# A copy of V into unit order during the mixing stage, and whole-row loads in the V stage

## The reference, cut to what matters

```python
q = einsum('bsd,dhe->bshe', h, w_q)             # 8 heads, two halves of 128
s1, s2 = (q halves) . k1, k2                    # 128 scores a side
top_s, ids = best 16 of the 16 x 16 sums        # experts out of 128*128 = 16384
gates = softmax(top_s)
act = gelu(einsum('td,thkd->thk', h, u[ids]))   # u: (16384, 1024)
out = einsum('thk,thkd->td', gates * act, v[ids])  # v: (16384, 1024)
```

## Time and profile before

| what | value |
|---|---|
| median of the timed runs | 1936.13 us |
| the profiled execution, its own time | 1935.26 us |
| its span in the profile | 1933.3 us |
| PE busy | 1852.7 us, 96% of the span |
| DVE / ACT / POOL busy | 1277.3 / 754.3 / 1135.8 us |
| moved by transfers | 360.89 MB, mean 187 GB/s |

### The profile page before, as it was taken

One profiled execution on the slowest core, in us unless ns is written; L12 is line 12 of the kernel. 1 busy time (PEld: TensorE's weight loads), 2 busy tenths in 40 slices (PEclk: granted clock), 3 DMA queues, 4 the chain that ended last, 5 costly groups with the idle time before them and its releaser, 6 DMA issues.

```text
span 1933.3 us, 24277 instructions
## 1 busy us (share of the span) xinstructions
PE 1852.7 (96%) x9045; PEld 1611.5 (83%) x9045; DVE 1277.3 (66%) x2244; ACT 754.3 (39%) x1190; POOL 1135.8 (59%) x666
## 2 busy tenths in 40 slices
PE   6999999989999999999999999988899989999987
PEld 5777788878888888888888888888899989989976
DVE  6355422357899778888989860137686867787543
ACT  5433322333232344444444442433343434344331
POOL 6322344433354476766767764478888888886420
PEclk9999999989999999999999999999999999999998
DMA  5211122312244435544454546649999999999501
GB/s 195 79 66 66 57 99 95 120 66 88 93 146 149 145 124 211 185 174 174 181 202 174 176 173 240 219 161 317 324 344 335 316 350 331 322 344 374 175 33 44
DMA packets 186484, 360.89 MB, mean 187 GB/s; under 512 B 16384, under 2 KB 122880, under 8 KB 184704
## 3 DMA queue, kind: packets, MB, share of 16 engines
q1 hardware_dynamic: 142304, 231.76, 35.8%
q0 software_dynamic: 22528, 67.19, 9.4%
q10 hardware_dynamic: 21536, 60.40, 8.4%
HBM read 298.44 MB, written 60.82 MB: 186 GB/s over the span
## 4 chain that ended last, share of the span: by engine, by line
PE 74%; POOL 17%; issue 3%; DMA 3%; DVE 2%; ACT 1%; ACTq 0%; SPq 0%; DVEq 0%
PE bank L744 36%; PE bank L552 11%; PE bank L554 10%; PE bank L553 10%; POOL wl L491 7%; POOL picked L519 6%; PE bank L769 2%; DMA raw<-stream 2%; POOL rows_ex L526 2%; POOL gout L526 1%; POOL rows_h L526 1%; PE bank L648 1%; PE bank L668 1%; PE bank L722 1%; PE bank L638 0%
## 5 line engine op out<-in xcount | busy, mean ns | idle before, releaser
L491 POOL TENSOR_TENSOR wl<-raw,wh 128x1024 fp32r<-128x1024 f32 x298 | 737.9, 2478 | 670.8 <-ACT wh L846 669.6
L846 ACT ACTIVATE wh<-raw 128x1024 fp32r<-128x1024 f32 x338 | 356.6, 1056 | 324.4 <-PE bank L554 269.1
L552 PE MATMUL bank<-hh,wh 128*128 128x512 f32 (+1 forms) x1056 | 394.5, 374 | 26.4 <-DVE x L1399 17.5
L744 PE MATMUL bank<-hh,wh 128*128 128x512 f32 x1024 | 400.5, 391 | 0.8 <-ACT scores L1001 0.8
L744 PE MATMUL bank<-hh,wl 128*128 128x512 f32 x1024 | 401.0, 392 | 0.0
L744 PE MATMUL bank<-hl,wh 128*128 128x512 f32 x1024 | 399.7, 390 | 0.0
L554 PE MATMUL bank<-hh,wl 128*128 128x512 f32 (+1 forms) x1056 | 387.7, 367 | 0.0
L553 PE MATMUL bank<-hl,wh 128*128 128x512 f32 (+1 forms) x1056 | 387.4, 367 | 0.0
L552 PEld LDWEIGHTS bank<-hh,wh 128*128 128x128 f32 x1056 | 201.3, 191 | 56.0 <-DVE x L1399 19.4
L744 PEld LDWEIGHTS bank<-hh,wl 128*128 128x128 f32 x1024 | 192.2, 188 | 37.7
L744 PEld LDWEIGHTS bank<-hl,wh 128*128 128x128 f32 x1024 | 192.4, 188 | 36.9
(11 more groups left out here) (211 smaller groups left out, 2569.7 us busy)
## 6 DMA issues: line engine op xcount, KB each, us to landing
raw<-stream SPq DMA_DIRECT2D x338, 512.0 KB, 3.7
score_dram<-gout ACTq DMA_DIRECT2D x128, 256.0 KB, 2.5
gate_dram<-stage ACTq DMA_DIRECT2D x12, 2048.0 KB, 7.5
gate<-gate_dram SPq DMA_DIRECT2D x16, 1536.0 KB, 12.7
score_in<-score_dram SPq DMA_DIRECT2D x64, 384.0 KB, 10.5
x<-xT SPq DMA_DIRECT2D x4, 512.0 KB, 5.6
picked<-score_dram,score_at POOLq DMA_INDIRECT x128, 6.1
outT<-outb SPq DMA_DIRECT2D x8, 256.0 KB, 2.1
```

The source lines that it names most:

```text
L491: nc.gpsimd.tensor_tensor(wl[:, n % SL, :], raw[:, n % RAW, :], wh[:, n % SL, :].bitcast(F32), ALU.subtract).then_inc(lo_done, 1)
L552: nc.tensor.matmul(out, ah, bh, start=start, stop=False)
L744: last = nc.tensor.matmul(psum[u % 2][:], w(weights, U_DENSE + u, c), tokens[c][:, :], start=c == 0 and which == 0, stop=c == DC - 1 and w ...
L846: nc.scalar.activation(wh[:, n % SL, :], raw[:, n % RAW, :], ACT.Copy).then_inc(hi_done, 1)
```

## The change

The kernel gets a new tensor in device memory, `v_units`, with 128 tiles in the order and shape of the V units. During units 6 to 69 SP issues two copies from `stream` to `v_units` ahead of each load, 128 copies of 512 KB in all. They wait for nothing. The first load of the V stage waits for all copies, and each V unit is then loaded from `v_units` as 128 rows of 4 KB.

```diff
+        v_units = nc.dram_tensor("v_units", (NK, P, UW), F32, kind="Internal").ap()
+        v_copied = sem("v_copied")
...
+            def copy_unit(m):
+
+                g, dp, hb = m // GB, m % GB // 2, m % 2
+                first = U_V0 + GB * g + HB * hb
+                part = stream[first:first + HB, :, 2 * P * dp:2 * P * (dp + 1)]
+                sp.dma_start(v_units[m].rearrange("p (j d) -> p j d", j=HB), part.rearrange("j p d -> p j d")).then_inc(v_copied, 16)
+
             for n in range(N_UNITS):
                 m = n - U_V0
+                for k in range(NK):
+                    if U_MIX + 2 + k // 2 == n:
+                        copy_unit(k)
...
                 if n >= RAW:
                     wait_low(sp, n - RAW)
+                if n == U_V0:
+                    sp.wait_ge(v_copied, 16 * NK)
                 if U_V0 <= n < U_PLE:
-                    g, dp, hb = m // GB, m % GB // 2, m % 2
-                    first = U_V0 + GB * g + HB * hb
-                    part = stream[first:first + HB, :, 2 * P * dp:2 * P * (dp + 1)]
-                    sp.dma_start(raw[:, n % RAW, :].rearrange("p (j d) -> p j d", j=HB),
-                                 part.rearrange("j p d -> p j d")).then_inc(raw_in[n % RAW], 16)
+                    sp.dma_start(raw[:, n % RAW, :], v_units[m]).then_inc(raw_in[n % RAW], 16)
                 else:
                     sp.dma_start(raw[:, n % RAW, :], stream[n]).then_inc(raw_in[n % RAW], 16)
```

## The result

The changed kernel takes 1941.76 us, the median of 20 runs (1938.67 to 1947.48), against 1936.66 for the kernel before on the same chips (20 runs, 1930.96 to 1939.76). The ratio is 1.0027, with a 95% interval of 1.0019 to 1.0034: 5.1 us slower by the medians, just over the 0.2% bound. The direction is as forecast. The size is not (12 us were forecast), and its terms are further off than the total, because the costs and the gain were both forecast too high and partly cancel.

A forecast was written before the change was run, and what follows sets the result against it. PE was taken to bound the merge stage; in the V stage transfers were short, with POOL nearly as short. 1935.3 + 9.6 (start) + 7.6 (norm) + 2 (clock) - 7 (V stage) = 1947.5, say 1947 us; 8-in-10 range 1925 to 1992.

The forecast's parts named there:

- The cost of a copy: SP's queue: c, the time of all 16 engines for one 512 KB copy, 1.5 to 2.9 us, taken as 2.4.
- the first rival: Copies overlap reading and writing, c of 1.5 to 1.9: 1929 to 1933 us, say 1931; chance 0.28.
- the start: Start of mixing: loads up to unit 10 stand behind ten copies, so PE is 9.6 us late at c = 2.4.
- the norm: Last square before the norm: loads of units 36 to 62 fall behind copies, delay 52c - 117.2, 7.6 us at c = 2.4.
- the 7 us of the V stage: V stage: loads of 4 KB rows save 11 to 15 us of transfer time, of which 7 us come through.
- its own signs of being wrong: U stage starting at its old place (c below 1.9) or over 50 us later, or V stage shrinking by over 18 us.
- the cover of 3.9 us: Start of mixing: slack between ACT's rounding of unit 10 with the `v_sb` copies behind it and PE's next projection.
- 10c - 14.45: Start of mixing: PE's delay in us from ten copies of cost c ahead of unit 10's load, 9.6 at c = 2.4.
- Clock: PE's clock falls to half when PE stands still; 2 us added for the longer stops.
- two bounds: V stage gain: nothing if POOL decides throughout, 17.5 us if POOL never waits.
- The last rival: V loads land no sooner because gates, scores and rows hold the queue; copies' cost stands alone, 1954 us; chance 0.12.
- The wait on `v_copied`: First V load, issued at 1203.25: copies end at 425 at the earliest or some tens of us later, so no cost.

The follow-up runs named there:

- the late: Changed kernel with the copies ahead of units 16 to 79 instead of 6 to 69: 1941.17 us, ratio 1.0023 to the kernel before.

## Why the prediction was right in direction and wrong in size

- **The cost of a copy was the step that failed.** Between 1.5 and 2.9 us I took 2.4, with the argument that the memory has to serve both ends. It measures 1.55 us in the changed kernel, where the queue has gaps, and 1.52 where it is full, so in these runs the writing adds next to nothing to the reading. 1 KB of a copy takes 46 ns at the median, and so does 1 KB of a load. This was the first rival, given 0.28. At c = 1.55 the prediction's own sums give 1 us for the start and nothing for the norm.
- **The direction came out right by luck in part.** With the measured cost of a copy and everything else as forecast, the sum is the first rival's, 1929 to 1933 us, which is faster than before. Slower it became because the 7 us of the V stage did not come and because of a cost that the prediction didn't have. One of its own signs of being wrong was the start of the U stage at its old place, with c below 1.9; unit 72 starts 3.6 us late, and c is below 1.9.
- The Trainium skill's number for copies between HBM tensors ("DMA: Bandwidth & Descriptors", section "Latency and other measured facts"), 207 GB/s per direction, is exceeded here. 0.524 MB in 1.55 us of all engines is 338 GB/s per direction. As moved in fact, with each copy made twice, the copies alone came to 36.3 MB in 264 to 390, 288 GB/s per direction, with loads beside them. The measurement decides; by the page's number the time would have been 1956, and it was 1941.76.
- **The start: mechanism right.** The path (loads behind copies, ACT's `v_sb`, PE's projection) is the one that the trace shows, and the cover of 3.9 us is confirmed: unit 10 is 5.6 us late and PE 1.7, and with twice the copies 21.2 and 17.3. The sum 10c - 14.45 gives 1.0 at c = 1.55. Without the copies there the step is gone.
- **The norm: 7.6 us forecast, 0 measured**, because of c. By that sum (52c - 117.2) a delay begins at c = 2.25 us. Doubling the copies brought a delay of the size of the sum, but most of it earlier, in the merge stage.
- **Clock: 2 us forecast for the longer stops.** In this profile two stops of 2.2 us each brought 3.4 us of half clock, 1.7 us a time, 3.4 in all. The term was there and about of the right size, but at stops that were much shorter than I had in mind. It isn't certain either: with the copies unused, a stop of 2.63 us brought none.
- **Not foreseen: the 2 KB transfers of another queue.** I counted who stands behind the copies in SP's queue, and not who shares the 16 engines with them. It cost 1.5 to 1.8 us of waiting and the second of the half clocks. By the trace it is half of the loss before the norm.
- **The V stage: 7 us forecast, 0 measured.** The saving of transfer time is there, and larger than I had it (21 us against 11 to 15). That half of it would come through was a compromise between two bounds, and the result lies at the lower one. I had POOL's row, with 510.5 of 528 us of work, and read the remaining 17.5 us as room; whole rows without copies show that no more than 3 us of it was to be had. The last rival (no gain in the V stage, the copies' cost alone) had that outcome at 0.12, with another reason for it.
- **The wait on `v_copied`: nothing, as forecast.** The copies are done hundreds of microseconds before 1203.

So the forecast of +12 was 9.6 + 7.6 + 2 - 7, and what the trace shows is 1.7 + 0 + 3.4 (clock) + 1.5 (the 2 KB transfers) - 0 = 6.6 before the norm, where the table has 6.3. At the end the two profiles are 6.0 us apart, after 2.7 us less at the norm and 2.4 us more in the V stage, and the medians say 5. These last differences are of the size by which the time at half clock varies between executions; no run here assigns them.

## What to carry to other kernels

An engine with 97% of a stage's time in its own work and issue is the first suspect for that stage's pace, whatever the waits of the others for transfers say. Here taking work from it was the only thing that helped, though just half of it came through. Relieve such an engine first, and try by itself the part of a change that is to bring the gain before paying for the part that prepares it. When transfers are put into idle capacity, list not only what is queued behind them but every small transfer of any queue that something waits for in that stretch. A copy from memory to memory costs here what a load of the same size costs, and can be hidden where units come slowly enough. And before a view's sum of waits is compared with another trace's, look at what stands under `issue` in both.

## What the runs showed of the hardware

- A 512 KB copy within device memory, in 1 KB pieces, took 1.52 to 1.56 us of all 16 engines in 250 to 390 (by its packets), and a load of 512 KB in 4 KB rows in the same stretch 1.52 us without copies beside it and 1.53 to 1.75 with them. In the V stage, where the engines are full, 512 KB loaded in 1 KB pieces took 1.64 us and in 4 KB rows 1.47.
- A 2 KB transfer on ACT's queue took 5.1 to 5.4 us to land with the engines full of copies from SP's queue, and 2.0 to 2.7 us otherwise.
- Behind copies, SP's issuing instruction itself took longer; SP at the start of mixing, after:

```profile
21.54 0.33 SPq L463 DMA_DIRECT2D raw<-stream  x1
...
38.35 1.55 SPq L463 DMA_DIRECT2D raw<-stream  x1
...
50.05 3.43 SPq L463 DMA_DIRECT2D raw<-stream  x1
```

No cost of its own shows: with twice the copies the sum of the queue alone gave c = 1.50 to 1.6, where the packets give 1.52.

- Stops of PE of 2.2 to 2.5 us were followed by 3.4 us at 1.2 GHz in four cases (two in the changed kernel, one each with the late and the unused copies), so each cost 1.7 us more than its length. A fifth, of 2.63 us, was not.
